# Chunk steps of a two-layer hybrid decoder: parts of the step take other places in the engines' order

## The chip, the cores and the metric

The kernel runs on one core of one Trainium2 chip. The metric is the time of one execution on the device in microseconds (us); lower is better. The engines are TensorE (PE, with its weight loads as PEld), VectorE (DVE), ScalarE (ACT), GpSimd (POOL) and SyncE (SP), which issues nearly all transfers.

## What is computed

One inference step of a two-layer decoder trunk in float32, for 1024 prompt tokens and 32 new tokens of 8 other sequences. Per layer:

```
parts = split(x @ w_in)                            # 2560 columns, three groups of heads
ret   = rmsnorm(retention(rq, rk, rv)) * silu(rg)                       # 4 heads
hg    = rmsnorm(hgrn2(hq, k, hi, logf)) * hg_norm_w * silu(hgt)         # 4 heads, k and logf from sigmoid(hf)
swa   = softmax_with_sink(q k^T / 8, window 128) v                      # 8 query heads, 2 key heads
x = layernorm(ALPHA * x + concat(ret, hg, swa) @ w_out)
x = layernorm(ALPHA * x + relu(x @ w_up)**2 @ w_down)
```

Retention and HGRN2 are scans over chunks of 128 tokens: each chunk needs the state that the chunk before it left. The new tokens start from given states and from a cache of 128 keys and values.

## The kernel before

Every matrix product of the projections is made of three float32r products of a high and a low part (hi*hi, hi*lo, lo*hi). So each weight that is loaded is first cast into its high part by ScalarE, and then GpSimd (for some VectorE) subtracts to get the low part. The products are those of lines 1089 to 1091.

Per layer there is a projection (`project`), the mixer (`mix`), the output projection (`attend_out`) and the two feed-forward products. The mixer is where the change is. It works in ten steps, 0 to 9, over nine chunks: eight of the prompt and, as the ninth, the new tokens ("decode"). In step s each engine has three chunks in hand: `g` = chunk s + 1, whose gates are made; `f` = chunk s, whose rotated queries and keys, window attention and decay levels are made ("front"); and `h` = chunk s - 1, whose HGRN2 and retention heads are finished ("heads"). In each step some pieces of dense work are put between: `dense(step, place)`, with places a1, a2, b, c, d, e. Table `PLACES` says how many units each has. In steps 0 to 4 they are "late units" of the input projection (tiles 5 to 8), with their results stored to memory by SyncE and loaded again as chunks; in steps 5 to 8 they are units 0 to 7 of the output projection: one at a1 and one at c in steps 5 to 7, one at a1 and one at d in step 8.

Every engine's order is written out by hand, in a `mix_step(step)` for each engine (TensorE at line 1477, ScalarE at 1957, VectorE at 2577, GpSimd at 3022, and SyncE's `step` at 911). An engine runs its instructions in order and waits on semaphores that others step.

What the change and the prediction speak of:

- TensorE: `front_transposes` (rotated queries and keys), `heads_keys` and `heads_weights` (level products L1267; L1256 is the small product for the diagonal and waits until ScalarE has copied the transposed keys of the next chunk, `front_copies`, from the same bank), `front_scores` for waves A and B of four heads each, `heads_out`, `window_weights` A and B (transposes of the probabilities), `gate_transposes(g)` (which waits until `cat_h` has been made from bank 0), `window_out`, and `heads_transposed`.
- ScalarE: `window_exps` and `window_norm` (L1893, L1900), `dense(step, "c")` (L1797 copies a late unit for its store; for an output unit L2016 makes the high part of the next output weight and L2021 collects the unit), `window_weights` (copies of the transposed probabilities, L1905 and L1908), `gates_sigmoid` (L1835 to L1843), `window_high`, `heads_high`, `gates_log` (L1847, after VectorE's step f1), and at the end of step 4 `split_wo(l, 0)`, the first output weight's high part.
- VectorE: `gates_sigmoid` (the clip L2329, then after ScalarE's exponentials L2332, L2336 and L2339, whose last step is f1), `window_low` (L2567) and `heads_low` (L2574), which subtract the high parts of the mixed rows, `front_queries`, `heads_keys` (g_kt, L2366), `gates_clip` (L2347), `heads_weights` (diag L2372, `hg_a` L2374, seven merges L2383), `front_silu` (L2478, L2479: the output gates), `front_levels` (scans L2395 and 14 subtractions), `front_masks` for waves A and B (L2430), `heads_rstd`, `window_sums`, and `heads_merge` (L2499, then the state updates L2511 and L2517, then the merged rows `cat_h`, L2504).
- GpSimd: `values`, `rotate(g)`, `levels`, `gate_weights`, and the low parts: `split_late` (L3055) and `split_wo` (L3060). Tables say in which step each falls:

```
OUT_BEFORE = {5: 1, 6: 3, 7: 5, 8: 7}
OUT_AFTER = {4: (0,), 5: (2,), 6: (4,), 7: (6,), 8: (8,)}
```

- SyncE: `next_h(s + 2)` loads the rows of the chunk after next. It waits for GpSimd's rotation and values and for the silu products of chunk s, since the buffer is theirs (`gg`, "s1"). In step 4 the order is: `next_v(5)`, the stores of the last late units (place c), a wait until they have landed, the loads of output weights 0 and 1, then `next_h(6)`.

Of the kernel before, what the change touches and what calls it, by code (L numbers as in the profile page):

```python
# [217 lines left out]
def build(nc, A):  # L218
    ctx = ExitStack()
    with ctx:  # L220
# [862 lines left out]
        def _(pe):  # L1083
# [120 lines left out]
            def mix(l):  # L1204
# [272 lines left out]
                def mix_step(step):  # L1477
                    g, f, h = chunk_at(l, step + 1), chunk_at(l, step), chunk_at(l, step - 1)
                    if f:
                        front_transposes(f, chunk_at(l, step - 2))  # L1480
                    if h:
                        heads_keys(h)
                        heads_weights(h, f)
                    dense(step, "a1")
                    dense(step, "a2")
                    if f and f.prompt:
                        front_scores(f, h, "A")
                        front_ret(f, h)
                    elif f:
                        front_ret(f, h)  # L1490
                        decode_keys(f, h)
                    if h:
                        heads_out(h, f)
                    dense(step, "b")
                    if f and f.prompt:
                        front_scores(f, h, "B")
                        dense(step, "c")
                        window_weights(f, h, "A")
                        window_weights(f, h, "B")
                        if g:  # L1500
                            gate_transposes(g, f, h)
                        dense(step, "d")
# [230 lines left out]
        def _(act):  # L1733
# [98 lines left out]
            def mix(l):  # L1832
# [124 lines left out]
                def mix_step(step):  # L1957
# [18 lines left out]
                    if f and f.prompt:  # L1976
# [3 lines left out]
                        dense(step, "c")  # L1980
# [12 lines left out]
                    if f and f.prompt and g:  # L1993
                        gates_log(g)
                    if step == 4:
                        split_wo(l, 0)
# [188 lines left out]
        def _(dve):  # L2185
# [131 lines left out]
            def mix(l):  # L2317
# [8 lines left out]
                def gates_sigmoid(c):  # L2326
# [3 lines left out]
                                    ALU.mult, ALU.min).then_inc(gc.step("clip"), 1)  # L2330
                    dve.wait_ge(gh.sem, gh.at("r", c.n))
# [162 lines left out]
                def heads_merge(c):  # L2494
# [6 lines left out]
                    if c.prompt:  # L2501
                        heads_states(c)
                    dve.wait_ge(md.sem, md.at("sr", c.n))
                    v.tensor_tensor(cat_h[0:rows, :], ps[0:rows, 0, :], gate[c.p][0:rows]  # L2504
                                    .rearrange("p a b -> p (a b)"), ALU.mult).then_inc(md.step("rh"), 1)

# [70 lines left out]
                def mix_step(step):  # L2577
                    g, f, h = chunk_at(l, step + 1), chunk_at(l, step), chunk_at(l, step - 1)
                    if f:
                        front_queries(f)  # L2580
                    if h:
                        heads_keys(h)
# [6 lines left out]
                    if f:  # L2589
                        front_silu(f)  # L2590
# [16 lines left out]
                    if h:  # L2607
                        heads_rstd(h)
                    if f and f.prompt:
                        window_sums(f, "B")  # L2610
                    if h:
                        heads_merge(h)
                    if f and f.prompt:
                        if g:
                            gates_sigmoid(g)
                        window_low(f)
# [4 lines left out]
                    if h:  # L2621
# [3 lines left out]
                gates_sigmoid(chunk_at(l, 0))  # L2625
                v.memset(st_r[:], 0.0).then_inc(zd.step("r"), 1)
# [257 lines left out]
        def _(pool):  # L2884
# [4 lines left out]
            def mix(l):  # L2889
# [132 lines left out]
                def mix_step(step):  # L3022
                    g, f, h = chunk_at(l, step + 1), chunk_at(l, step), chunk_at(l, step - 1)
                    if f:
                        values(f, h)
                        for G in LOW_BEFORE.get(step, ())[:1]:
# [5 lines left out]
                    if f:  # L3032
# [9 lines left out]
                        for out in OUT_AFTER.get(step, ()):  # L3042
                            split_wo(l, out)
# [97 lines left out]
```

## Time and profile before

| what | us |
|---|---|
| median of 3 runs | 2735.28 |
| lowest and highest | 2732.26, 2736.43 |
| the profiled execution | 2732.12 |
| its span, first to last instruction | 2730.3 |
| TensorE busy in the span | 2555.8 (94%) |
| VectorE busy | 1680.6 (62%) |
| ScalarE busy | 836.7 (31%) |
| GpSimd busy | 997.7 (37%) |

The first mixer lies at about 182 to 559 us of the span, the second at about 1536 to 1905 us. Busy shares over the whole span are means over stages of different kinds: the products of the feed-forward part fill TensorE, the mixer does not. The rows below are from the first layer; the second shows the same pattern, shifted.

### The profile page before, as it was taken

To read this page: it belongs to the slowest core of one execution; us is meant where nothing else is said; L and a number is where in the kernel's file an instruction comes from. 1 tells how busy PE (TensorE), PEld (TensorE's weight loads), DVE (VectorE), ACT (ScalarE), POOL (GpSimd) and SP (SyncE) were. 2 spreads that over 40 slices of the span, in tenths; PEclk is the share of its full clock that TensorE was granted. 3 is DMA by queue.
4 is the path that set the end of the run, shared out by engine and by line. 5 is a ranking of instruction groups with operands and counts; after the bars stand their busy time and mean duration, and the time that the engine had idled before them with its cause. 6 is when DMAs were issued, how large, how long until landed. Compare 5 with 4: busy or idle time off the path is not lost. (4 is left out here: it accounts for less than half of the span.)

```text
span 2730.3 us, 45275 instructions
## 1 busy us (share of the span) xinstructions
PE 2555.8 (94%) x18126; PEld 2366.2 (87%) x18126; DVE 1680.6 (62%) x3361; ACT 836.7 (31%) x1667; POOL 997.7 (37%) x1052
## 2 busy tenths in 40 slices
PE   7999988789999999999899999887999999999996
PEld 7998866588999999999899987666989999999996
DVE  3136678558855666666851367884596555666668
ACT  3235665232322221111122455661322222111110
POOL 0027666531555531122000466664325555222220
PEclk9999999789999999999999999997999999999998
DMA  4442232162233253223343531321622233432323
GB/s 168 148 157 88 90 108 54 34 197 82 80 108 113 95 181 94 92 93 95 109 146 130 166 105 57 106 69 40 196 76 95 95 123 116 158 95 91 94 79 112
DMA packets 225889, 295.83 MB, mean 108 GB/s; under 512 B 28817, under 2 KB 177617, under 8 KB 225649
## 3 DMA queue, kind: packets, MB, share of 16 engines
q1 hardware_dynamic: 225680, 292.94, 33.5%
q8 instruction: 144, 2.36, 0.4%
q14 instruction: 65, 0.52, 0.1%
HBM read 217.27 MB, written 77.66 MB: 108 GB/s over the span
## 5 line engine op out<-in xcount | busy, mean ns | idle before, releaser
L1089 PE MATMUL ps<-hid_hi,wd_hi 128*128 128x256 f32 (+2 forms) x800 | 257.5, 322 | 12.7 <-DVE acc_b L2778 6.7
L1090 PE MATMUL ps<-hid_lo,wd_hi 128*128 128x256 f32 (+2 forms) x800 | 255.3, 319 | 0.0
L1089 PE MATMUL ps<-hid_hi,wdl_hi 128*128 128x256 f32 (+2 forms) x800 | 255.2, 319 | 0.0
L1090 PE MATMUL ps<-hid_lo,wdl_hi 128*128 128x256 f32 (+2 forms) x800 | 255.1, 319 | 0.0
L1091 PE MATMUL ps<-hid_hi,wd_lo 128*128 128x256 f32 (+2 forms) x800 | 255.1, 319 | 0.0
L1091 PE MATMUL ps<-hid_hi,wdl_lo 128*128 128x256 f32 (+2 forms) x800 | 254.8, 318 | 0.0
L2762 DVE TENSOR_TENSOR acc_a<-ps,acc_a 128x512 f32<-128x512 f32 x208 | 143.9, 692 | 152.3 <-PE ps L1091 152.3
L3077 POOL TENSOR_TENSOR wq_lo_S<-ws,wq_hi_S 128x512 fp32r<-128x512 f32 x104 | 199.1, 1923 | 104.3 <-ACT wq_hi_S L2087 104.3
L2762 DVE TENSOR_TENSOR acc_b<-ps,acc_b 128x256 f32<-128x256 f32 (+1 forms) x416 | 178.2, 439 | 74.2 <-PE ps L1091 69.2
L3055 POOL TENSOR_TENSOR wl_lo<-wl_raw,wl_hi 128x2048 fp32r<-128x2048 f32 x14 | 63.8, 4558 | 415.7 <-ACT wl_hi L1789 415.6
L1089 PE MATMUL ps<-wi_hi,u_hi 128*128 128x320 f32 x600 | 185.7, 309 | 2.1 <-DVE wi_lo L2273 2.1
L1090 PE MATMUL ps<-wi_lo,u_hi 128*128 128x320 f32 x600 | 186.3, 311 | 0.0
L1091 PE MATMUL ps<-wi_hi,u_lo 128*128 128x320 f32 x600 | 185.5, 309 | 0.0
L1089 PE MATMUL ps<-wl_hi,u_hi 128*128 128x256 f32 (+1 forms) x640 | 182.2, 285 | 2.1 <-ACTq L598 1.1
L1090 PE MATMUL ps<-wl_lo,u_hi 128*128 128x256 f32 (+1 forms) x640 | 179.9, 281 | 0.0
L1089 PE MATMUL ps<-t_hi_T,wq_hi_S 128*128 128x256 f32 (+1 forms) x624 | 177.7, 285 | 1.7 <-issue 1.7
L1091 PE MATMUL ps<-wl_hi,u_lo 128*128 128x256 f32 (+1 forms) x640 | 178.9, 280 | 0.0
L1090 PE MATMUL ps<-t_lo_T,wq_hi_S 128*128 128x256 f32 (+1 forms) x624 | 178.3, 286 | 0.0
L3086 POOL TENSOR_TENSOR wdl_lo<-wd_raw,wdl_hi 128x1024 fp32r<-128x1024 f32 x32 | 78.5, 2480 | 270.8 <-ACT wdl_hi L2046 270.8
L1091 PE MATMUL ps<-t_hi_T,wq_lo_S 128*128 128x256 f32 (+1 forms) x624 | 177.4, 284 | 0.0
L3086 POOL TENSOR_TENSOR wd_lo<-wd_raw,wd_hi 128x1024 fp32r<-128x1024 f32 x32 | 76.5, 2417 | 266.0 <-ACT wd_hi L2046 259.9
L1089 PEld LDWEIGHTS ps<-hid_hi,wd_hi 128*128 128x128 f32 x800 | 151.8, 190 | 24.7 <-DVE acc_b L2778 7.0
(329 smaller groups left out, 7872.2 us busy)
## 6 DMA issues: line engine op xcount, KB each, us to landing
wd_raw<-in_w_down SPq DMA_DIRECT2D x32, 1024.0 KB, 4.9
wq_raw<-in_w_up SPq DMA_DIRECT2D x26, 1024.0 KB, 6.1
wl_raw<-in_w_in SPq DMA_DIRECT2D x20, 1024.0 KB, 5.1
wi_raw<-in_w_in SPq DMA_DIRECT2D x15, 1280.0 KB, 6.6
hidscr<-h SPq DMA_DIRECT2D x32, 544.0 KB, 7.9
out_y<-xn SPq DMA_DIRECT2D x32, 512.0 KB, 4.6
hidscr<-h SPq DMA_DIRECT2D x32, 512.0 KB, 7.1
hid_raw<-hidscr SPq DMA_DIRECT2D x32, 512.0 KB, 3.5
```

The source lines that it names most:

```text
L1089: nc.tensor.matmul(out, a_hi, b_hi, start=start, stop=False)
L1090: nc.tensor.matmul(out, a_hi, b_lo, start=False, stop=False)
L1091: return nc.tensor.matmul(out, a_lo, b_hi, start=False, stop=stop)
L2762: v.tensor_tensor(at, got, at, ALU.add).then_inc(down_free, 1)
L3055: g_.tensor_tensor(wl_lo[G % 2][:], wl_raw[G % 2][:], wl_hi[G % 2][:], ALU.subtract)\
L3077: g_.tensor_tensor(wq_lo[m][:], w_quarter(m), wq_hi[m][:], ALU.subtract).then_inc(wq_lo_done, 1)
L3086: g_.tensor_tensor(lo[:, :, cols], wd_raw[:, :, cols], hi[:, :, cols], ALU.subtract).then_inc(wd_lo_done, 1)
```

## The change

- TensorE: `gate_transposes(g)` stands between `window_weights` A and B instead of behind B.
- ScalarE: from step 4 on, `dense(step, "c")` stands behind `heads_high` and `gates_log` instead of before `window_weights`.
- VectorE: `gates_sigmoid` is cut in two, the clip and `gates_keys`, called one right after the other. In `heads_merge` the state updates follow `cat_h` instead of preceding it. `heads_low` of a prompt chunk is done in the next step, behind `front_queries`. `front_silu` is done behind `heads_rstd` instead of before `front_levels`.
- GpSimd: the low part of an even output weight (`OUT_AFTER`) is made in the next step, behind `values` and after a wait for VectorE's f1, instead of at the end of its own step.

```
--- before.py
+++ after.py
@@ -1496,9 +1496,9 @@
                         front_scores(f, h, "B")
                         dense(step, "c")
                         window_weights(f, h, "A")
-                        window_weights(f, h, "B")
                         if g:
                             gate_transposes(g, f, h)
+                        window_weights(f, h, "B")
                         dense(step, "d")
                         window_out(f)
                     elif f:
@@ -1977,7 +1977,8 @@
                         window_exps(f, "B")
                         window_norm(f, "A")
                         window_norm(f, "B")
-                        dense(step, "c")
+                        if step < 4:
+                            dense(step, "c")
                         window_weights(f)
                         if g:
                             gates_sigmoid(g)
@@ -1992,6 +1993,8 @@
                         heads_high(h)
                     if f and f.prompt and g:
                         gates_log(g)
+                    if f and f.prompt and step >= 4:
+                        dense(step, "c")
                     if step == 4:
                         split_wo(l, 0)
                     if step == CHUNKS:
@@ -2328,6 +2331,9 @@
                     dve.wait_ge(hpe.sem, hpe.at("h", c.n))
                     v.tensor_scalar(g_e[:], ps[:, 0, 0:256].rearrange("p (a b) -> p a b", a=2), -1.0, 80.0,
                                     ALU.mult, ALU.min).then_inc(gc.step("clip"), 1)
+
+                def gates_keys(c):
+                    dve.wait_ge(gc.sem, gc.at("clip", c.n))
                     dve.wait_ge(gh.sem, gh.at("r", c.n))
                     v.tensor_tensor(g_e[:], g_e[:], g_r[:], ALU.mult).then_inc(gc.step("s"), 1)
                     dve.wait_ge(gc.sem, gc.at("s", c.n))
@@ -2498,11 +2504,11 @@
                     both = gate[c.p][0:rows].rearrange("p a (h d) -> p (a h) d", h=4)
                     v.tensor_tensor(both, both, rms[0:rows].unsqueeze(2).broadcast_to([rows, 8, 64]), ALU.mult)\
                         .then_inc(md.step("sr"), 1)
-                    if c.prompt:
-                        heads_states(c)
                     dve.wait_ge(md.sem, md.at("sr", c.n))
                     v.tensor_tensor(cat_h[0:rows, :], ps[0:rows, 0, :], gate[c.p][0:rows]
                                     .rearrange("p a b -> p (a b)"), ALU.mult).then_inc(md.step("rh"), 1)
+                    if c.prompt:
+                        heads_states(c)
 
                 def heads_states(c):
                     dve.wait_ge(mpe.sem, mpe.at("st", c.n))
@@ -2576,8 +2582,11 @@
 
                 def mix_step(step):
                     g, f, h = chunk_at(l, step + 1), chunk_at(l, step), chunk_at(l, step - 1)
+                    past = chunk_at(l, step - 2)
                     if f:
                         front_queries(f)
+                    if past:
+                        heads_low(past)
                     if h:
                         heads_keys(h)
                     if f:
@@ -2587,7 +2596,6 @@
                     if h:
                         heads_weights(h)
                     if f:
-                        front_silu(f)
                         front_levels(f)
                         if f.prompt:
                             front_masks(f, "A")
@@ -2606,6 +2614,8 @@
                         window_sums(f, "A")
                     if h:
                         heads_rstd(h)
+                    if f:
+                        front_silu(f)
                     if f and f.prompt:
                         window_sums(f, "B")
                     if h:
@@ -2613,16 +2623,17 @@
                     if f and f.prompt:
                         if g:
                             gates_sigmoid(g)
+                            gates_keys(g)
                         window_low(f)
                     elif f:
                         decode_window(f)
                     if h and not h.prompt:
                         decode_states_h(h)
-                    if h:
                         heads_low(h)
 
                 split_late(1)
                 gates_sigmoid(chunk_at(l, 0))
+                gates_keys(chunk_at(l, 0))
                 v.memset(st_r[:], 0.0).then_inc(zd.step("r"), 1)
                 v.memset(st_h[:], 0.0).then_inc(zd.step("h"), 1)
                 v.memset(lev_r[:], 0.0).then_inc(zd.step("lr"), 1)
@@ -3023,6 +3034,13 @@
                     g, f, h = chunk_at(l, step + 1), chunk_at(l, step), chunk_at(l, step - 1)
                     if f:
                         values(f, h)
+                    if step - 1 in OUT_AFTER:
+
+                        if f:
+                            pool.wait_ge(gc.sem, gc.at("f1", f.n))
+                        for out in OUT_AFTER[step - 1]:
+                            split_wo(l, out)
+                    if f:
                         for G in LOW_BEFORE.get(step, ())[:1]:
                             split_late(l, G)
                         if step in OUT_BEFORE:
@@ -3039,8 +3057,6 @@
                         gate_weights(f)
                         for G in LOW_AFTER.get(step, ()):
                             split_late(l, G)
-                        for out in OUT_AFTER.get(step, ()):
-                            split_wo(l, out)
                     if h:
                         heads(h)
```

## Rows read from the trace of the kernel before

**Rows 1.** Steps 5, 6: us; PE, PEld, DVE, ACT, POOL busy; clock, DMA share, GB/s.

```profile
376.84:410.75 33.91, 29.72 (x168) 23.39 (x169) 26.07 (x76) 20.09 (x51) 26.34 (x44) 0.95 0.44 136
410.75:445.77 35.02, 28.55 (x169) 21.77 (x168) 28.79 (x83) 21.05 (x53) 24.02 (x43) 1.00 0.17 47
```

**Rows 2.** Waits of TensorE in steps 6 and 7: total us, times, longest us.

```profile
PE ps L1085 <- ACT prob L1900: 3.5, 4, 1.3
PE ps L1427 <- ACT probT L1908: 3.0, 2, 1.5
PE ps L1267 <- DVE u_lo L2567: 2.9, 2, 1.4
```

**Rows 3.** Timeline, ScalarE and TensorE, step 6: start us, duration us, instruction, idle before.

```profile
439.98 1.03 ACT L2016 CAST wo_hi<-wo_in_lo 128x1024 fp32r<-128x1024 f32 x1
441.39 1.00 ACT L1905 COPY probT<-ps 128x1024 f32<-128x1024 f32 x1
442.30 1.06 ACT L1908 COPY probT<-ps 128x512 f32<-128x512 f32 x2
...
440.13 1.09 PE L1085 MATMUL ps<-ident,prob 128*128 128x128 f32 x8 [0.51 <-ACT prob L1900]
```

**Rows 4.** L2332's durations (ns, min/median/max); VectorE's timeline, steps 5, 6.

```profile
L2332 DVE TENSOR_TENSOR g_e<-g_e,g_r x18: 426/738/2009, 178.2 to 1832.8; 128x256 f32<-128x256 f32 x18
...
409.58 2.01 DVE L2332 TENSOR_TENSOR g_e<-g_e,g_r 128x256 f32<-128x256 f32 x1 [2.21 <-ACT g_r L1839]
416.60 0.16 DVE L2372 COPY diag<-ps 128x4 f32<-128x4 f32 x1 [1.19 <-PE ps L1256]
421.36 0.59 DVE L2478 TENSOR_TENSOR gate<-hb,gate 128x256 f32<-128x256 f32 x1
422.47 1.22 DVE L2395 TENSOR_TENSOR_SCAN g_b<-const,g_r 128x128 f32<-128x128 f32 x2
436.92 0.33 DVE L2445 TENSOR_TENSOR den<-ssum,esk 128x4 f32<-128x4 f32 x1 [1.03 <-ACT esk L1895]
```

**Rows 5.** Timeline of GpSimd, steps 5 and 6.

```profile
408.94 2.36 POOL L3060 TENSOR_TENSOR wo_lo<-wo_in_lo,wo_hi 128x1024 fp32r<-128x1024 f32 x1
418.56 2.41 POOL L3060 TENSOR_TENSOR wo_lo<-wo_in_lo,wo_hi 128x1024 fp32r<-128x1024 f32 x1 [6.48 <-ACT wo_hi L2016]
```

**Rows 6.** Timeline of ScalarE, end of step 4 and start of step 5.

```profile
369.02 0.61 ACT L1797 COPY l_out<-ps 128x256 f32<-128x256 f32 x2
374.93 0.42 ACT L1847 ACTIVATE g_r<-g_r 128x256 f32<-128x256 f32 x1 [0.23 <-DVE g_r L2339]
375.92 1.04 ACT L2016 CAST wo_hi<-wo_in_lo 128x1024 fp32r<-128x1024 f32 x1 [0.58 <-DMA wo_in_lo<-in_w_out]
378.76 0.27 ACT L1860 COPY r_kT<-ps 128x128 f32<-128x128 f32 x1 [1.79 <-DVE r_qi L2361]
```

**Rows 7.** Timeline: TensorE and VectorE in step 5; VectorE and GpSimd in step 2.

```profile
381.31 0.51 PE L1256 MATMUL ps<-const,g_p 128*128 128x2 f32 x4
382.05 0.69 DVE L2374 TENSOR_TENSOR hg_a<-ident,diag 128x512 f32<-128x512 f32 x1
...
263.76 2.65 DVE L2347 TENSOR_SCALAR gate<-hb 128x256 f32<-128x256 f32 x2
260.99 4.53 POOL L3055 TENSOR_TENSOR wl_lo<-wl_raw,wl_hi 128x2048 fp32r<-128x2048 f32 x1 [1.13 <-ACT wl_hi L1789]
```

**Rows 8.** Timeline of step 1: VectorE, SyncE, ScalarE.

```profile
249.91 0.29 DVE L2445 TENSOR_TENSOR den<-ssum,esk 128x4 f32<-128x4 f32 x1 [1.19 <-ACT esk L1895]
253.71 0.42 SPq L718 DMA_DIRECT2D wl_raw<-in_w_in  x1
259.01 1.91 ACT L1789 CAST wl_hi<-wl_raw 128x2048 fp32r<-128x2048 f32 x1 [0.97 <-DMA wl_raw<-in_w_in]
```

**Rows 9.** Landing of loads: late weights, then chunk rows.

```profile
DMA to landing us min/median/max: 4.9/5.1/9.8
DMA to landing us min/median/max: 2.0/3.6/6.2
```

More of the change, by code:

```diff
@@ L1979, in mix_step @@
                         window_norm(f, "B")
-                        dense(step, "c")
+                        if step < 4:
+                            dense(step, "c")
                         window_weights(f)
@@ L1994, in mix_step @@
                         gates_log(g)
+                    if f and f.prompt and step >= 4:
+                        dense(step, "c")
                     if step == 4:
@@ L2330, in gates_sigmoid, with gates_keys @@
                                     ALU.mult, ALU.min).then_inc(gc.step("clip"), 1)
+                def gates_keys(c):
+                    dve.wait_ge(gc.sem, gc.at("clip", c.n))
                     dve.wait_ge(gh.sem, gh.at("r", c.n))
@@ L2505, in heads_merge @@
                                     .rearrange("p a b -> p (a b)"), ALU.mult).then_inc(md.step("rh"), 1)
+                    if c.prompt:
+                        heads_states(c)
                 def heads_states(c):
@@ L2578, in mix_step @@
                     g, f, h = chunk_at(l, step + 1), chunk_at(l, step), chunk_at(l, step - 1)
+                    past = chunk_at(l, step - 2)
                     if f:
                         front_queries(f)
+                    if past:
+                        heads_low(past)
                     if h:
@@ L2589, in mix_step @@
                     if f:
-                        front_silu(f)
                         front_levels(f)
@@ L2608, in mix_step @@
                         heads_rstd(h)
+                    if f:
+                        front_silu(f)
                     if f and f.prompt:
@@ L2615, in mix_step @@
                             gates_sigmoid(g)
+                            gates_keys(g)
                         window_low(f)
@@ L2625, in mix @@
                 gates_sigmoid(chunk_at(l, 0))
+                gates_keys(chunk_at(l, 0))
                 v.memset(st_r[:], 0.0).then_inc(zd.step("r"), 1)
@@ L3025, in mix_step @@
                         values(f, h)
+                    if step - 1 in OUT_AFTER:
+                        if f:
+                            pool.wait_ge(gc.sem, gc.at("f1", f.n))
+                        for out in OUT_AFTER[step - 1]:
+                            split_wo(l, out)
+                    if f:
                         for G in LOW_BEFORE.get(step, ())[:1]:
@@ L3041, in mix_step @@
                             split_late(l, G)
-                        for out in OUT_AFTER.get(step, ()):
-                            split_wo(l, out)
                     if h:
```

5 lines of the change are left out of this document (1 added, 4 removed).

## The prediction

> **What bounds the kernel now.** The profiled execution took 2732.12 us, of which the span is 2730.3; the median shown is 2735.28, 3.2 above it. The sum below is made on the profiled one and the difference is carried to the median. About 0.2% (5.5 us) is what a measurement of this kernel can tell from no change.
>
> I read the busy time by stretch first. The change touches only the chunk steps. Step 6 lasts 35.0 us and TensorE is busy for 28.6 of them [rows 1]: there it is not the bound. The longest waits of TensorE over steps 6 and 7 [rows 2] name ScalarE's scaled probabilities (L1900), its copies of the transposed ones (L1908) and VectorE's `window_low` (L2567): a chain that goes to and fro between VectorE and ScalarE. In steps 0 to 3 more late units fill TensorE, and VectorE waits for it; little on VectorE or ScalarE can pay there.
>
> The chain in step 6 is: levels, masks B, exponentials, scaled probabilities, then on ScalarE the copy of an output weight, the collected unit, the copies of the transposes [rows 3], the gate exponentials, then on VectorE L2332 to L2339 and `window_low`, and in the next step `diag` (L2372), its merges, the two silu products and the levels again [rows 4].
>
> **Part by part, steps 5 to 7.**
>
> (a) `front_silu` leaves the place before the levels. It takes from 421.36 to 422.47, 1.1 us [rows 4], on the chain. Its new place is where VectorE idles 1.03 us for ScalarE, before 436.92 [rows 4]. Gain 1.1 a step; if GpSimd's level products slow it further, up to 0.5 less.
>
> (b) `dense(step, "c")` on ScalarE goes behind the logs. From 439.98 to 441.39 it stands before the copies of the transposes, 1.4 us. TensorE ends wave B's transposes at 441.22, so the copy that starts at 442.30 could start at 441.3 [rows 3]. Gain 1.0 (0.7 to 1.4). TensorE's gate transposes move into the 0.5 us that it waits between the two waves, and `cat_h` before the states gives them their bank in time; both are needed for this 1.0 and give nothing more here. `heads_low` moves behind `front_queries`; window_low, queries, low part and g_kt stay on VectorE before the same reader, so it is zero, with 0.3 either way.
>
> (c) The low part of an even output weight leaves the end of GpSimd's step. It runs 408.94 to 411.30 [rows 5], and L2332, issued at 409.58, takes 2.01 us where the fastest of 18 takes 0.43 [rows 4]. So 1.6 us are there to win; the small GpSimd operations that now fall beside L2332 to L2339 take some back. I take 0.9 (0.3 to 1.6).
>
> (d) Now what it will meet. It starts when ScalarE has made the high part, some 1.5 us after f1, and VectorE reaches `gates_clip` about 1 us later. Two clips beside a long GpSimd subtraction took 2.65 us at 263.76, until it was over [rows 7]; here they would end 0.35 us after `diag` is ready, since `diag` waits 1.19 us today [rows 4]. Cost 0.35 (0 to 1.9).
>
> (e) The odd weight's subtraction (418.56, 2.41 us [rows 5]) and the rotation behind it hardly move, while VectorE's levels come 2 us earlier. The scans (L2395) then begin under the subtraction (0.6) and the last levels lose their undisturbed end (0.3): 0.9 (0 to 1.5).
>
> A full cycle therefore gains 1.1 + 1.0 + 0.9 - 0.35 - 0.9 = 1.75. From masks B of step 5 to those of step 7 there are two. From step 7 to 8 only (b) and (c) count, 1.9, since step 8 waits for TensorE. Together 5.4 per layer.
>
> **Step 4 to 5.** This is the term that speaks against the change. Today ScalarE copies the last two late units at 369.02 and finds the first output weight at 375.92, 6.9 us later, after a wait of only 0.58 [rows 6]: SyncE stores those units, waits until they have landed and only then loads the weight, all beside other work. After the change the copies come behind the log of 374.93, at 375.2. The weight then comes at 382.1, and ScalarE, in order, idles until then; `front_copies` (378.76 today) follows at 383.1. TensorE's L1256 needs them for its bank: 383.5 instead of 381.31 [rows 7], +2.2. The weight's low part on GpSimd then runs 383.1 to 385.5, over `hg_a` (L2374, 0.69 us [rows 7]). No row shows that line beside such a subtraction; the nearest is L2332, also with two operands in SBUF, which ended 0.29 after it [rows 4, 5]. I take +1.3 by it, with 0 as the other end. (a) gives back 1.1, undisturbed levels cost 0.2, and TensorE's clock, 0.95 in this stretch against 1.00 in the next [rows 1], falls for a second idle time: 0.2. Cost 2.2 + 1.3 - 1.1 + 0.2 + 0.2 = 2.8 (1.0 to 4.5).
>
> The Trainium skill ("SBUF — State Buffer", Who interferes with whom) says that VectorE and GpSimd share a pair of ports as an exclusive lock, that an operation with two SBUF inputs takes part, and that the later one blocks for the whole instruction. By it the 1.3 stands; without it the sum would be 2.6 us better over both layers. L2332 agrees.
>
> **Steps 0 to 3.** Step 0 is bound by TensorE, and the gate transposes in its 0.5 us wait give 0.4. In steps 1 and 2 that gain is lost in a wait for a late weight, and here the silu move has a cost. SyncE loads the chunk after next only when silu is done. In step 1 silu would end at 249.8 (VectorE's idle time begins at 249.91 - 1.19 [rows 8], plus 1.1). The four loads of a chunk and its values then run until about 256.5 (a piece of `hb` lands up to 6.2 us after its issue [rows 9]). The late weight is issued at 253.71, and ScalarE waits for it at 259.01, with `window_high`, `window_low` and TensorE's levels behind it [rows 8]. Landing took 5.1 us as a rule and 9.8 at most [rows 9]; behind 1.3 MB of other loads I take +1.4 here and +1.1 in step 2. Cost 2.5 per layer (0 to 5). Step 0 has slack for the same effect, and step 3 loads no chunk.
>
> The skill's "DMA: Bandwidth & Descriptors" (Anatomy of one DMA) fits about 2.0 us plus bytes over 436 GB/s. By that figure, as an estimate, both loads, 2.4 MB, would be there 7.5 us after 249.8, before 259.01, and the 2.5 would be zero; the usual landing of 5.1 us for 1 MB, where it gives 4.4, is slower than the page.
>
> **Other steps.** In step 8 silu stands behind the root, 0 to 1.1; GpSimd's subtraction there blocks the later s_prob product anyway, so 0.1. Splitting `gates_sigmoid` puts no instruction elsewhere: zero. State updates behind `cat_h` are ready 0.7 us later, several us before the next transposes of q ask for them: zero; without that cover 0.7. In step 7 SyncE's load of weight 6 waits for silu too, 13 us later than today, but its reader has moved behind the logs as well: zero, up to 2 if it lands late.
>
> **Sum.** Per layer +0.4 - 2.5 - 2.8 + 5.4 - 0.1 = 0.4 us gained, 0.8 over both: 2731.3 on the profiled execution, 2734.5 against the median. Forecast: no change that can be measured.
>
> **The rivals.**
>
> Faster: the chunk's load and the late weight's fit side by side, the 2.5 is zero. For it speaks that SyncE's queues stand idle most of a step; against it that two late weights issued together landed 9.8 us after issue [rows 9]. Per layer 2.9, 5.8 over both: 2729.5; with the cycles at 2.5 each in place of 1.75 another 3.0, 2726.5. This is also where the page's figure leads.
>
> Slower: GpSimd's subtractions catch VectorE in steps 5 to 7. It decides in `gates_clip` and the first scan: if the even one starts 1 us later than I have it, the clips and then `hg_a` wait for it whole (1.3 instead of 0.35), and the scans for the odd one (1.5 instead of 0.9); (c) stays at its lower end, 0.3. A full cycle then gains nothing (1.1 + 1.0 + 0.3 - 1.3 - 1.5 = -0.4) and the last 1.3, so a layer loses 4.5: 9 us slower, 2744. It decides for slower than 0.2% once a full cycle gains under 0.2. The lengths of L2332 and of the clips in step 2 speak for it; that GpSimd idles 6.48 us before the odd one [rows 5] speaks against it.
>
> Off the path: TensorE or a transfer bounds all steps. TensorE's idle 6.5 us in step 6 [rows 1] speaks against it: 2735.3.
>
> **Numbers.** No change 0.40, the off-path case with it; faster by over 0.2% 0.36; slower by over 0.2% 0.24, which holds, beside the rival, a hand-over of 4.5 with late weights 5 late. All terms at their good ends give 11 us faster, all at their bad ends far more slower, but they are hardly one case: 2725 to 2743. The forecast's own range is 2730 to 2740.
>
> **What would show it.** In the trace after: ScalarE idle 5 to 6 us before the first output weight at the end of step 4, and step 5 longer by 2 to 4 us; step 6 at 33.3 instead of 35.0, step 7 a little less; L2332 at 0.4 to 0.9 in all steps; `hg_a` of step 4's heads near 2 us; VectorE's clips near 2 us in steps 6 to 8; ScalarE's wait for the late weight in steps 1 and 2 longer by 1 to 2 us. Steps 6 and 7 under 32.5, or that wait unchanged, would make it wrong on the fast side; steps of 35 on the slow side.

## The result and the profile after

The change made the kernel slower: 2744.85 us median over 20 runs (2734.25 to 2754.37) against 2738.82 for the kernel before, also 20 runs (2729.94 to 2749.36), ratio 1.0026 [1.0014, 1.0037]. The forecast was no measurable change, 2734.5, and the range (2725 to 2743) ended below the measured time. Forecast and range stood on the three runs shown before, median 2735.28; the 20 runs have 2738.82, 3.5 higher. Counted from the kernel before, the forecast was 0.8 us less and the measured change is 6.0 us more, clear of noise. That the time itself lies above the range owes something to the low base; that it went up does not.

Rows from here on have each kernel's own line numbers, a few higher than those of the kernel before in the changed ones: L2338 is L2332 of the kernel before (the gates' product), L2353 is L2347 (the clips), L2380 is L2374 (`hg_a`), L2401 is L2395 (the scans), L2573 is L2567 (`window_low`), L3076 is L3060 (the low part of an output weight).

The two profiled executions lie further apart than the medians (spans 2730.3 and 2746.8), so they show where time can go and the ratios say how much on average. Stretches of the kernel before, steps 2, 3, 6 and 7 of the first layer and steps 2 and 3 of the second (columns as in [rows 1]: us; PE, PEld, DVE, ACT and POOL busy; granted clock, DMA share, GB/s):

```profile
259.90:302.30 42.40, 38.65 (x290) 34.14 (x289) 28.64 (x82) 24.16 (x58) 27.55 (x42) 0.96 0.30 99
302.30:341.70 39.40, 36.83 (x289) 32.43 (x288) 26.86 (x78) 23.34 (x58) 26.80 (x40) 1.00 0.16 52
410.70:445.80 35.10, 28.63 (x170) 21.85 (x169) 28.87 (x83) 21.13 (x53) 24.11 (x43) 1.00 0.17 47
445.80:480.80 35.00, 28.51 (x170) 21.80 (x169) 28.76 (x83) 21.05 (x53) 24.00 (x43) 1.00 0.24 59
1613.40:1655.50 42.10, 36.97 (x289) 32.46 (x288) 30.74 (x82) 25.03 (x58) 27.66 (x42) 1.00 0.31 100
1655.50:1695.00 39.50, 36.94 (x289) 32.50 (x288) 26.93 (x78) 23.39 (x58) 26.87 (x41) 1.00 0.16 52
```

The same stretches of the changed kernel, with step 5 (382.70) of the first layer:

```profile
259.40:303.20 43.80, 38.12 (x289) 33.92 (x288) 28.59 (x80) 24.06 (x57) 27.57 (x42) 0.96 0.29 93
303.20:347.70 44.50, 39.93 (x290) 35.40 (x289) 27.69 (x81) 24.28 (x58) 27.37 (x41) 0.92 0.16 54
382.70:417.50 34.80, 30.06 (x168) 23.55 (x169) 27.75 (x78) 19.62 (x49) 25.00 (x45) 0.95 0.45 139
417.50:451.00 33.50, 28.38 (x170) 21.81 (x169) 30.69 (x83) 21.29 (x53) 24.10 (x44) 1.00 0.24 70
451.00:484.50 33.50, 28.37 (x170) 21.79 (x168) 30.69 (x83) 21.28 (x53) 24.09 (x44) 1.00 0.22 51
1614.30:1659.30 45.00, 39.84 (x289) 35.53 (x288) 31.68 (x82) 24.21 (x57) 27.79 (x42) 0.92 0.28 88
1659.30:1704.00 44.70, 39.13 (x289) 34.91 (x288) 26.98 (x78) 24.22 (x58) 27.06 (x40) 0.92 0.17 54
```

Steps 6 and 7 went from 35.1 and 35.0 to 33.5, as forecast (33.3). Steps 2 and 3 went from 42.4 + 39.4 and 42.1 + 39.5 to 43.8 + 44.5 and 45.0 + 44.7: 6.5 and 8.1 us longer, where 2.5 were forecast. Their clock (0.96 and three times 0.92, against 0.96 and three times 1.00) is the mean of stretches at 2.4 GHz and at 1.2. One profile is no measure of that: kernels further down that leave silu at its old place in these steps also show some of them at 0.92 (experiment 11 in its second layer: 44.8 and 43.1 us, both at 0.92). But over all the profiles the two groups stay apart. The changed kernel and experiments 3, 5, 7 and 9, with silu late and the loads in that order, have a mean clock of 0.933 to 0.945 in these four steps, which together last 175 to 181 us; the kernel before and the eight others have 0.951 to 0.990 and 163 to 169 us. The timeline of the changed kernel at the end of step 1 (SPq is SyncE's issue, the bracket is idle time and what ended it):

```profile
249.78 1.27 SPq L738 DMA_DIRECT2D hb<-hscr  x3
251.56 0.91 SPq L744 DMA_DIRECT2D hv<-hscr  x2
253.75 0.42 SPq L718 DMA_DIRECT2D wl_raw<-in_w_in  x1
261.31 1.90 ACT L1789 CAST wl_hi<-wl_raw 128x2048 fp32r<-128x2048 f32 x1 [3.79 <-DMA wl_raw<-in_w_in]
263.72 0.69 DVE L2573 TENSOR_TENSOR u_lo<-ps,u_hi 128x512 fp32r<-128x512 f32 x1 [5.45 <-ACT u_hi L1912]
264.47 3.57 PE L1267 MATMUL ps<-lev_r,lev_x 128*128 128x128 f32 x16 [3.93 <-DVE u_lo L2573]
```

Against [rows 8]: the late weight is issued when it was (253.75, before 253.71), but behind the chunk's rows, which start at 249.78 (forecast 249.8). ScalarE's wait for it is 3.79 us instead of 0.97, and TensorE waits 3.93 us at its level products, where the kernel before has

```profile
262.17 1.16 PE L1267 MATMUL ps<-lev_r,lev_x 128*128 128x128 f32 x8 [1.11 <-DVE u_lo L2567]
```

The hand-over of step 4 to 5, changed kernel, beside [rows 6, 7]:

```profile
380.34 0.61 ACT L1797 COPY l_out<-ps 128x256 f32<-128x256 f32 x2
387.07 1.04 ACT L2019 CAST wo_hi<-wo_in_lo 128x1024 fp32r<-128x1024 f32 x1 [6.11 <-DMA wo_in_lo<-in_w_out]
388.50 0.61 PE L1256 MATMUL ps<-const,g_p 128*128 128x2 f32 x4 [1.15 <-ACT s_kT L1861]
389.34 1.83 DVE L2380 TENSOR_TENSOR hg_a<-ident,diag 128x512 f32<-128x512 f32 x1
```

ScalarE stands idle 6.11 us, the small product waits for the copy of the keys, and `hg_a` takes 1.83 us instead of 0.69. All three were foreseen. Step 5 is longer by 0.9 us in the first layer (33.9 to 34.8) and by 2.9 in the second (33.5 to 36.4), where 2 to 4 were forecast.

Step 6 of the changed kernel on VectorE and GpSimd, beside [rows 4, 5]:

```profile
420.62 1.99 DVE L2353 TENSOR_SCALAR gate<-hb 128x256 f32<-128x256 f32 x2
427.29 1.84 DVE L2401 TENSOR_TENSOR_SCAN g_b<-const,g_r 128x128 f32<-128x128 f32 x2
449.87 0.92 DVE L2338 TENSOR_TENSOR g_e<-g_e,g_r 128x256 f32<-128x256 f32 x1 [1.79 <-ACT g_r L1839]
...
419.90 2.36 POOL L3076 TENSOR_TENSOR wo_lo<-wo_in_lo,wo_hi 128x1024 fp32r<-128x1024 f32 x1 [2.13 <-ACT wo_hi L2019]
425.62 2.41 POOL L3076 TENSOR_TENSOR wo_lo<-wo_in_lo,wo_hi 128x1024 fp32r<-128x1024 f32 x1 [3.36 <-ACT wo_hi L2019]
```

The clips take 1.99 us (0.48 before) and end just after the even subtraction, the scans begin under the odd one (1.84 instead of 1.22), and the gates' product takes 0.92 instead of 2.01.

And the place that the prediction priced at 0.1 us, VectorE's scaling of the decode probabilities in step 8, with the subtraction on GpSimd and TensorE behind it:

```profile
514.40 3.72 DVE L2557 TENSOR_SCALAR s_prob<-s_prob,rden 128x160 f32<-128x160 f32 x2
514.78 2.34 POOL L3076 TENSOR_TENSOR wo_lo<-wo_in_lo,wo_hi 128x1024 fp32r<-128x1024 f32 x1
518.17 1.12 PE L1085 MATMUL ps<-ident,s_prob 128*128 128x128 f32 x4 [8.12 <-DVE s_prob L2557]
```

The kernel before has 3.24 us and a wait of 4.87 at this place in the first layer, and 1.01 and 3.91 in the second.

### The profile page after: what moved, and what is told of

It is laid out like the page before. It is cut to its first block and busy times, and to the rows that moved or that the text cites. A ratio compares the mean times of both kernels' runs of the same rounds, so it can differ in the third digit from the quotient of the medians.

```text
span 2746.8 us, 45301 instructions
## 1 busy us (share of the span) xinstructions
PE 2561.3 (93%) x18126; PEld 2373.8 (86%) x18126; DVE 1701.3 (62%) x3361; ACT 838.3 (31%) x1667; POOL 998.9 (36%) x1052
## 3 DMA queue, kind: packets, MB, share of 16 engines
q1 hardware_dynamic: 225680, 292.94, 33.5%
```

## The experiments

Each kernel was timed in five rounds beside the kernel before on the same chip; the ratio is to that kernel, with its 95% interval. One per mille is 2.74 us. A difference between two of the ratios carries the scatter of both, some 2 to 3 per mille either way. Where a kernel has only 6 or 7 runs, it is said; the others have 11 or 12.

**1. Silu back at its old place, everywhere** (changed kernel):

```
                     if f:
+                        front_silu(f)
                         front_levels(f)
...
-                    if f:
-                        front_silu(f)
```

> The changed kernel with front_silu back before front_levels in every step. Theory A (the loss is the silu move in steps 1 and 2: the chunk load issued behind it delays the late weight, TensorE's longer wait then drops its clock): the starts of steps 2 to 4 lie 82 us apart as in the kernel before (88 and 90 in the changed one), steps 5 to 7 lose 1.1 each again, 34.6 instead of 33.5; against the changed kernel about 14 us less and 6 us more, so 8 us faster than it, ratio to before 0.9995 (0.998 to 1.001). Theory B (the loss is the hand-over from step 4 to 5): steps 2 and 3 count little, ratio stays at 1.003 or gets worse, 1.005.

2734.23 us, 0.9984 [0.9968, 1.0001]: 4.2 per mille (11.5 us) below the change. In the first layer of its profile the late weight lands 5.1 and 5.9 us after issue (7.5 and 6.6 in the changed kernel), and steps 6 and 7 last 33.9. So the new place of silu is worth 0.4 us there and costs far more elsewhere.

**2. Only SyncE's order mended** (changed kernel, silu stays late):

```
-                    if s != 3 and s + 2 < TILES:
+                    if s != 3 and s + 2 < TILES and s not in (1, 2):
                         next_h(s + 2)
...
                             dense(s, place)
+                            if place == "c" and s in (1, 2):
+                                next_h(s + 2)
```

> The changed kernel, silu where the change puts it, but in steps 1 and 2 SyncE issues the loads of the chunk after next behind the stores and the late weight of place c, not before them. Theory A: it is the order of the transfers, so the late weight lands 5 us after issue, TensorE's wait before the levels is 1.1 again and steps 2 and 3 take 82 us together: about 13 us faster than the changed kernel, ratio to before 0.998 (0.996 to 1.000). If silu itself (VectorE's time in its new place) were what costs in steps 1 to 3: no change against the changed kernel, 1.0026. Theory B: 1.0026 too.

2735.66 us, 0.9994 [0.9975, 1.0013]: 3.2 per mille, some 9 us (13 were expected), by the order of the loads in two steps. Its timeline, SyncE and ScalarE:

```profile
253.04 0.43 SPq L718 DMA_DIRECT2D wl_raw<-in_w_in  x1
254.20 1.48 SPq L738 DMA_DIRECT2D hb<-hscr  x3
258.10 1.91 ACT L1791 CAST wl_hi<-wl_raw 128x2048 fp32r<-128x2048 f32 x1 [1.29 <-DMA wl_raw<-in_w_in]
```

The weight is there 5.1 us after its issue; behind the chunk's rows it took 7.5 (253.75 to 261.3).

**3. Only the hand-over mended** (changed kernel):

```
-                        if step < 4:
+                        if step < 5:
                             dense(step, "c")
...
-                    if f and f.prompt and step >= 4:
+                    if f and f.prompt and step >= 5:
                         dense(step, "c")
```

> The changed kernel with dense(step, c) on ScalarE moved from step 5 on instead of step 4 on. Theory B: ScalarE's idle time before the first output weight goes from 5 to 6 us to 0.6, step 5 begins as before and 2 to 3 us per layer come back: about 6 us faster than the changed kernel, ratio 1.000. Theory A: the same 2 to 3 us per layer at this place, but steps 2 and 3 stay at 88 to 90 us together, so the ratio stays above 1, 1.0005 (0.999 to 1.002).

2739.99 us, 1.0004 [0.9987, 1.0020]: 2.2 per mille, 6 us. Its profile has the same 6 us at the place: step 5 lasts 32.8 and 32.3 us in the two layers, in the changed kernel 34.8 and 36.4. ScalarE's wait for the first output weight is gone and `hg_a` takes 0.69 us in step 5:

```profile
380.91 0.42 ACT L1847 ACTIVATE g_r<-g_r 128x256 f32<-128x256 f32 x1 [0.59 <-DVE g_r L2345]
381.56 1.04 ACT L2019 CAST wo_hi<-wo_in_lo 128x1024 fp32r<-128x1024 f32 x1 [0.23 <-DMA wo_in_lo<-in_w_out]
```

**4. Both: silu late in steps 4 to 7 alone, the collected unit behind the logs from step 5** (`if step < 4 or step == 8` ahead of the early `front_silu`, its negation ahead of the late one, and the edit of experiment 3):

> Silu late only in steps 4 to 7, dense(step, c) behind the logs from step 5 on. If the gains of steps 5 to 7 (1.5 us per step, two mixers) and the two losses are independent terms: steps 2 and 3 at 82 us together, no idle ScalarE before the first output weight, steps 6 and 7 at 33.5: 10 us faster than before, ratio 0.996 (0.994 to 0.998). If the losses are one (only one of the two can be seen at a time): 0.999.

2722.90 us over 7 runs, 0.9939 [0.9913, 0.9965]: the fastest of the study, faster than both kernels, and by 17 us where 10 were expected. That is 8.7 per mille below the change, where experiments 1 and 3 gave 4.2 and 2.2; what the rest is, experiments 8 and 12 ask.

**5. The kernel before with silu late everywhere, and nothing else:**

```
-                        front_silu(f)
                         front_levels(f)
...
+                    if f:
+                        front_silu(f)
                     if f and f.prompt:
                         window_sums(f, "B")
```

> The kernel before with one edit: front_silu at its new place (behind the root of the heads, before wave B's sums) in every step; everything else as before. Theory A (the chunk load now stands ahead of the late weight in SyncE's queue in steps 1 and 2, the weight lands 1 to 2.5 us later, ScalarE, VectorE and TensorE wait for it, and TensorE's clock falls more often in steps 2 and 3) makes this edit alone cost most of what the whole change lost: landing of the weight 6.8 to 7.6 us after issue in steps 1 and 2, TensorE's wait for u_lo 3 to 4 us, about 6 us slower than before, less 0.4 per step 5 to 7 and layer that the products' absence before the levels gives (2.4 in all): ratio 1.000 to 1.003. Theory B (the loss is the hand-over of step 4 to 5) gives only the gain: 2.4 to 6.6 us faster, ratio 0.998 to 0.999, and step spacings of steps 1 to 3 as before.

2750.8 us (6 runs), 1.0051 [1.0033, 1.0069], worse than either theory gave. In step 7 SyncE loads the new tokens' states only when silu is done, and output weight 6 stands behind them in its queue. It is issued 28.0 us after the start of the step (at 454.9), in the kernel before 13.9 us after it:

```profile
482.92 0.89 SPq L780 DMA_DIRECT2D wo_in_lo<-in_w_out  x1
488.12 1.04 ACT L2016 CAST wo_hi<-wo_in_lo 128x1024 fp32r<-128x1024 f32 x1 [4.33 <-DMA wo_in_lo<-in_w_out]
```

Step 7 lasts 41.1 and 41.2 us (before: 35.0 and 33.4). In the changed kernel the cast had moved behind the logs and the late load was covered, as forecast; alone, the silu move costs it.

**6. Experiment 4 with GpSimd's even subtraction back at the end of its step:**

```
-                    if step - 1 in OUT_AFTER:
-                        if f:
-                            pool.wait_ge(gc.sem, gc.at("f1", f.n))
-                        for out in OUT_AFTER[step - 1]:
-                            split_wo(l, out)
...
+                        for out in OUT_AFTER.get(step, ()):
+                            split_wo(l, out)
```

> The best kernel so far (silu late only in steps 4 to 7, the collected unit behind the logs only from step 5) with GpSimd's low part of the even output weights back at the end of its step. My terms (c), (d), (e): L2338, the gates' product, goes from 0.9 back to about 1.6 to 2.0 us in steps 5 to 7 and the cycle grows by 0.2 to 1.1 us, 6 cycles: 1 to 6 us slower than with the new place, 2724 to 2729. If the new place is worth nothing (another chain sets the cycle), the steps 5 to 7 stay at 33.0 to 33.5 and the time stays at 2723. If the new place costs (its contention with the scans), 2718 to 2721.

2724.61 us (6 runs), 0.9946 [0.9925, 0.9966], not told apart from experiment 4. Steps 6 and 7 stay at 33.6 and 33.5. The edit hardly moves the subtraction: it starts some 2.4 us after the start of step 6 in both, since ScalarE's cast, which it waits for, now stands behind the logs. So L2338 stays at 0.88 us and the clips at 2.13. What the new place on GpSimd was meant to do, ScalarE's edit does by itself; experiment 10, with that edit alone, has

```profile
444.61 2.00 DVE L2332 TENSOR_TENSOR g_e<-g_e,g_r 128x256 f32<-128x256 f32 x1 [2.22 <-ACT g_r L1839]
449.96 0.48 DVE L2347 TENSOR_SCALAR gate<-hb 128x256 f32<-128x256 f32 x2
...
445.00 0.52 DVE L2335 TENSOR_TENSOR g_e<-g_e,g_r 128x256 f32<-128x256 f32 x1 [1.38 <-ACT g_r L1839]
448.80 2.20 DVE L2350 TENSOR_SCALAR gate<-hb 128x256 f32<-128x256 f32 x2
```

(first the kernel before, then experiment 10): the product gains 1.5 us and the clips lose 1.7.

**7. TensorE kept busy in its wait** (changed kernel, `front_transposes`):

```
+                    more = 4 if (c.n % TILES) in (2, 3) else 0
-                    for g in range(4):
+                    for g in list(range(4)) * (1 + more):
```

> The changed kernel, with TensorE's four transposes of q done five times over in steps 2 and 3 (16 more, 2.4 us, before the wait for u_lo, whose length the late weight sets, so that this wait falls from 3.9 to about 1.5 us and the levels start when they did). If TensorE's idle time itself is what brings its clock down to 1.2 GHz while the late units run in steps 2 and 3, the granted clock of these steps goes from 0.92 to 0.96 to 1.00 and the kernel gains 2 to 5 us over the changed one: 2738 to 2743. If the clock falls for another reason (the work before or after, the run), the steps' clocks and the time stay within the scatter: 2743 to 2747. The wait itself is not taken away, so the 2.3 us a step that it costs stay in either case.

2742.98 us, 1.0020 [1.0005, 1.0035] against 1.0026 for the change: unclear. The granted clock over the execution rose (mean of 12 runs 0.9716, of the changed kernel's 20 runs, taken at another time, 0.9697), but in its profile steps 2 and 3 still have 0.93, 0.93, 0.93 and 1.00. Whether the idle time itself brings the clock down stays open.

**8. Experiments 2 and 3 together:**

> The changed kernel with both mends but silu late in every step: in steps 1 and 2 SyncE issues the chunk load behind the late weight, and the collected unit stands behind the logs only from step 5. If load order and the hand-over of step 4 to 5 are the whole loss, this equals the best kernel (2723, within 5 us): steps 6 and 7 at 33.5, hg_a 0.69 us in step 5, the late weight landing in about 5 us. If the place of silu costs by itself in steps 0 to 3 and 8 (VectorE's products later on the way to u_lo or to the decode step), it stays 5 us or more above it, 2728 to 2733.

2728.9 us, 0.9972 [0.9957, 0.9988]. The two mends add up (3.2 and 2.2 of 5.4 per mille), and 3.3 per mille are missing to experiment 4, which has silu at its old place in steps 0 to 3 and 8. In its profile the scaling of the decode probabilities takes over 3 us in both layers, in experiment 4's 0.8:

```profile
504.98 0.77 DVE L2557 TENSOR_SCALAR s_prob<-s_prob,rden 128x160 f32<-128x160 f32 x2
507.10 2.35 POOL L3078 TENSOR_TENSOR wo_lo<-wo_in_lo,wo_hi 128x1024 fp32r<-128x1024 f32 x1
505.81 1.11 PE L1085 MATMUL ps<-ident,s_prob 128*128 128x128 f32 x4 [3.87 <-DVE s_prob L2557]
```

(experiment 4, step 8: the scaling ends before the subtraction begins, and TensorE's wait is 3.87 us.)

**9. The kernel before with silu late in steps 1 and 2 alone** (the edit of experiment 5 under `if step in (1, 2)`):

> The kernel before with front_silu at its new place in steps 1 and 2 alone. If SyncE's order of the chunk load and the late weight is the loss of the first steps, the late weight lands 6.8 to 7.6 us after its issue in these steps, TensorE's wait for u_lo grows by some 2 us in steps 2 and 3, the clock there falls a little more often, and the kernel is 4 to 8 us slower than before: ratio 1.0015 to 1.003. Steps 5 to 8 are as before (the 6 us of step 7 that the kernel with silu late everywhere showed are gone). If the loss of the first steps needed the other parts of the change, the ratio is within 0.999 to 1.001.

2747.46 us, 1.0028 [1.0014, 1.0041]: 7.6 us, as much as the whole change lost. The late weight of steps 1 and 2 lands 6.1 to 7.2 us after its issue (before: 4.9 to 6.2), and TensorE's four waits for it are 2.1 to 2.8 us (before: 1.1 to 2.0). Two of its stretches, step 2 of the first layer and step 3 of the second:

```profile
258.50:305.80 47.30, 41.56 (x290) 37.26 (x289) 31.86 (x82) 24.31 (x57) 27.57 (x42) 0.89 0.29 90
1668.70:1710.90 42.20, 38.59 (x289) 33.94 (x288) 27.06 (x78) 24.27 (x58) 27.07 (x41) 0.96 0.15 50
```

**10. The kernel before with ScalarE's collected unit behind the logs from step 5** (the edit of experiment 3 made there), **and 11. the same with TensorE's gate transposes between the waves and `cat_h` ahead of the state updates:**

> The kernel before with one edit: ScalarE's collected unit (and the cast of the output weight ahead of it) behind the logs from step 5. TensorE's and VectorE's order as before. By my prediction the edit needs the gate transposes between the two waves, since otherwise the gates' exponentials, which now come ahead, wait for TensorE; it then gives nothing or little: steps 5 to 7 at 34.5 to 35, 2735 to 2738. If it needs nothing else, the copies of the transposed probabilities start 1.0 to 1.4 us earlier and steps 5 to 7 come to 33.5 to 34: 2 to 4 us a layer, 2730 to 2734.

> As the kernel before it, with TensorE's gate transposes between the two waves and cat_h ahead of the state updates as well: my term (b) whole, without silu, without GpSimd's new place and without the new place of the low part. Term (b) gives 1.0 a cycle and 0.4 in step 0: 33.9 in steps 6 and 7, 2726 to 2731. If what made the best kernel 14 us faster lies elsewhere (GpSimd's place, the low part's place, the hand-over), this stays at 2733 to 2737; if it is all in these three edits, it is 2722 to 2726.

2728.18 us, 0.9962 [0.9946, 0.9978], and 2725.7 us (6 runs), 0.9952 [0.9936, 0.9968]. Steps 6 and 7 of the first layer last 34.0 in both. So the collected unit needs no other edit, against what my term (b) said; the two ratios are not told apart. These edits give most of what the best kernel has.

**12. Experiment 4 with silu late in step 8 too:**

```
-                        if step < 4 or step == 8:
+                        if step < 4:
                             front_silu(f)
...
-                    if f and not (step < 4 or step == 8):
+                    if f and not (step < 4):
                         front_silu(f)
```

> The best kernel so far with one edit: in step 8 front_silu is late again (as in the changed kernel), so that it stands late in steps 4 to 8. Theory C, from the traces: in step 8 the two products (1.1 us) stand ahead of VectorE's scaling of the decode probabilities, which then no longer ends before GpSimd's subtraction of an output weight begins; it takes 3.2 to 3.7 us instead of 0.8, TensorE waits 8 us instead of 4 for it, and the first cat_h transposes of step 8 come 39 us after the step's start instead of 34.5. Then this kernel shows these numbers in both layers and is 5 to 9 us slower than the best one: 2727 to 2732, ratio to before 0.996 to 0.998. By my prediction's step (0.1 us a layer) it stays at 2721 to 2725, ratio 0.993 to 0.995.

2729.11 us, 0.9983 [0.9970, 0.9996]: 4.4 per mille above experiment 4, intervals apart (each against its own runs of the kernel before). Both layers show the mechanism, and the first transposes of `cat_h` in step 8 come 39.1 us after the start of the step, in experiment 4 34.8 and 34.4. The first layer:

```profile
503.88 3.71 DVE L2557 TENSOR_SCALAR s_prob<-s_prob,rden 128x160 f32<-128x160 f32 x2
507.65 1.12 PE L1085 MATMUL ps<-ident,s_prob 128*128 128x128 f32 x4 [8.11 <-DVE s_prob L2557]
```

The two profiled executions differ by only 1.5 us in all (spans 2717.9 and 2719.4): the 9 us of step 8 are there, and experiment 4's profile lost most of them elsewhere. The price of 4.4 per mille rests on the ratios.

## Why the prediction was wrong

**The steps that held.** Steps 6 and 7 gained 3.1 us in the first layer (3.5 forecast for two cycles); in step 8 the first transposes of `cat_h` come 0.8 us sooner after the start of the step (39.2 against 40.0). The parts were less right than their sum. Term (b) measured 1.0 (35.0 to 34.0, experiments 10 and 11), but what I called needed for it is not. Term (a) gave 0.4 (33.9 to 33.5, experiment 1) and not 1.1: the odd subtraction, term (e), took 0.6 of it in the scans (1.21 us in experiment 1, 1.84 in the changed kernel). Terms (c) and (d), 0.55 together, were put down to GpSimd's edit, which gives nothing (experiment 6). What they describe comes with ScalarE's edit, and there the clips lose what the product gains.

**The hand-over** was forecast as 3.5 us a layer before the gains, 7.0 in all; mending it gave 2.2 per mille, 6 us, with some 5 us of scatter either way. The Trainium skill ("SBUF — State Buffer", Who interferes with whom), by which the later of two such operations blocks for the whole instruction, was the ground for 1.3 of it; `hg_a`, from 389.34 on beside the subtraction of 388.26 to 390.62, took 1.83 us, 1.14 longer, so the trace agrees (1.41 in the second layer).

**First failed step: "Steps 0 to 3", the late weight.** The mechanism was right to the tenth of a microsecond in its start (249.78), and the size was off: 2.5 us a layer forecast, 5 in all, against 7.6 (experiment 9), 8.8 (experiment 2) and 8.8 (experiment 8 against 3). Each of the three has an interval of 4 to 6 us either way, so one alone does not tell it from 5. The landing was a little later than I took it (in step 1 by 2.3 us where I took 1.4, in step 2 by 1.7 where I took 1.1). Above all the sum held nothing for TensorE's clock in steps 2 and 3. Where the clock is the same, the size is right: step 2 of the first layer, at 0.96 in both kernels, is 1.4 us longer. Each run comes with its span and its mean granted clock; over the 203 runs of all kernels but those taken with experiment 12, the span grows 1.9 us for each 0.001 of clock that is missing, within a kernel. The kernel before has a mean clock of 0.9713 (75 runs), the changed one 0.9697, experiment 9 has 0.9688. At equal clock (a fit with one slope for all and a level for each kernel) the change costs 4.8 us (standard error 0.9) and experiment 9 costs 4.8 (1.1); the rest, about 3 and 5 us, goes with the lower clock. The profiles say where: the mean over steps 2 and 3 is 0.938 in the five kernels with the late weight behind the rows and 0.971 in the nine others, which over some 165 us is 0.002 of the whole. There the clock is costly, because TensorE bounds these steps: it is busy 36.8 of 39.4 us in step 3 before, and 39.9 of 44.5 after at 0.92. How the cost divides is not firm: of experiment 2's gain nearly all, 8.7 us, remains at equal clock, and how a later weight brings the clock down is shown by no run (experiment 7 leaves it open).

The rival "Faster", and the page of the Trainium skill whose figure led there ("DMA: Bandwidth & Descriptors", Anatomy of one DMA: about 2.0 us plus bytes over 436 GB/s, fitted on GpSimd's kind of queue), had both loads there 7.5 us after the first issue. They were there after 11.5 (249.78 to 261.3). Of these, 4.0 passed before SyncE issued the weight at all, which that reading left out. From its issue on, the weight took 7.5 us, and the page's figure for 1 MB alone gives 4.4: the figure does not hold for this load on this queue behind the rows.

**Second failed step: "In step 8 silu stands behind the root [...] GpSimd's subtraction there blocks the later s_prob product anyway, so 0.1".** That was read from the first layer alone. In the kernel before:

```profile
512.03 3.24 DVE L2551 TENSOR_SCALAR s_prob<-s_prob,rden 128x160 f32<-128x160 f32 x2
...
1863.43 1.01 DVE L2551 TENSOR_SCALAR s_prob<-s_prob,rden 128x160 f32<-128x160 f32 x2
1864.99 2.35 POOL L3060 TENSOR_TENSOR wo_lo<-wo_in_lo,wo_hi 128x1024 fp32r<-128x1024 f32 x1
```

In the second layer the scaling is done before the subtraction begins. The front of my document said that the second layer shows the same pattern; here it does not. It is a race, and all 14 profiles can be read for it. With silu early in step 8 (the kernel before and experiments 1, 4, 6, 9, 10, 11) it was won in 10 of 14 layers: the scaling takes at most 1.4 us, TensorE's wait is 2.4 to 4.1 us, and the first transposes of `cat_h` come 34.3 to 35.8 us after the start of the step. The four lost ones are the first layers of the kernel before and of experiments 1, 6 and 9. With silu late, in the changed kernel and experiments 2, 3, 5, 7, 8 and 12, it was won in none of 14: the scaling takes over 3 us beside the subtraction or stands behind it, the wait is 5.2 to 8.1 us. In all 18 lost layers the transposes come at 38.7 to 40.0 us. So a lost race is some 4 to 5 us a layer, whatever silu does, and silu ahead of the scaling loses it. Against the kernel before, which had lost the first layer already, the changed kernel's profile is 0.8 us better there and 3.8 worse in the second (39.3 against 35.5): 3 us, where 0.2 were forecast. Against experiment 4, which won both, experiment 12 puts a price on it: 4.4 per mille between the two ratios, 12 us, of which 5 remain at equal clock; its profile shows 9 at the place.

**The account**, in per mille of the time: experiment 11 has -4.8, and with the rest of the change done where it helps, experiment 4 has -6.1. Silu late in step 8 adds 4.4 (experiment 12 against 4), or 3.3 with its late place in steps 0 to 3 as well (experiment 8 against 4), the loads' order 3.2, the hand-over 2.2: -6.1 + 3.3 + 3.2 + 2.2 = 2.6, and 2.6 was measured. The sum tests one thing, that the last two add up; each difference carries an interval of some 2 per mille or more, so that it comes out exactly is partly luck. Term (b) gave twice its forecast (6.8 us for it in all, about 13 measured in experiment 11, 3 us a layer of it in steps 5 to 7). The rest fits the race of step 8: experiments 10 and 11 win it in the first layer, where the kernel before lost it, and their `cat_h` comes 5.7 and 4.2 us sooner there. Nothing in these edits aims at that, and no run tells its share apart.

The rival "Slower" (subtractions catch VectorE in steps 5 to 7) had the right kind and the wrong place: the clips are held whole, as it said, and steps 6 and 7 still gained 1.5 each in the first layer. That its time, 2744, is nearly the measured 2744.85 is luck: it stood on the low base and on a loss in steps that gained.

## What to carry to other kernels

An edit that moves an instruction moves every transfer and every operation that waits for it: look what stands behind those transfers in their queue, and where TensorE bounds the step, compare the clock of the steps before and after, not only the wait. Where two engines race for a shared resource, read every instance of the race in the trace, the second layer too; a race won by half a microsecond before is a term, not a zero. A change of several moves is best timed move by move: here three edits made 13 us, and two others, silu's new place (11.5) and the collected unit's in step 4 (6), took more than that back.

## What the runs showed of the hardware

A 1 MB load on SyncE's queue was there 5.1 us after its issue with free queues and 7.5 us after it behind some 1.3 MB issued in the 4 us ahead. TensorE's clock went with small things: two products moved in two steps of each layer (experiment 9) came with a mean granted clock lower by 0.0025 (0.9688 against 0.9713), which goes with about 5 us, beside 4.8 us at equal clock. The runs of one kernel scatter by 0.3 to 0.4% to either side, and a good part of that goes with the clock: within the kernel before, clock and span correlate by -0.65 to -0.85 in each set of its runs. And a VectorE operation with one input in SBUF, the scaling by a column of 128x160 (0.3 to 0.6 us), took 3.0 to 3.3 us beside GpSimd's subtraction. The Trainium skill ("SBUF — State Buffer", Who interferes with whom) names this kind of operation among those that can take the ports shared with GpSimd; the trace agrees.
